# A fused two-block transformer kernel: mLSTM order, first feed-forward features, expert buffers and one set of modulation loads

## The reference

```
first_block:  cond = silu(c) @ w_ada + b_ada              # shifts, scales, gates ("modulation")
  layer 0:    x = layer_norm(ALPHA*x + gate * mlstm_layer(modulate(x)))          "ln00"
              x = layer_norm(ALPHA*x + gate * moe_ffn(modulate(x)))              "ln01"
  layer 1:    x = layer_norm(ALPHA*x + gate * moba_layer(modulate(x), kv))       "ln10"
              x = layer_norm(ALPHA*x + gate * moe_ffn(modulate(x)))              "ln11"
second_block, twice:
              x = x + 0.5 * swiglu(rms_norm(x) * ffn1)    # width 2816; "f10", "f11"
              x = x + three mixers of rms_norm(x) * mix, gated and merged
              x = x + 0.5 * swiglu(rms_norm(x) * ffn2)    # "f20", "f21"
mlstm_layer:  4 heads of 512; per head q, k, v, masked q.k weights, sum over values, a group norm
              over the head (mean, variance), then (norm*gn_g + skip*xc) * silu(z), then @ w_out
moe_ffn:      16 experts of 1024 x 512 (gate, up) and 512 x 1024 (down), top 2 for each token
```

## Time and profile before

| | us |
|---|---|
| median of 3 runs (2419.46 to 2423.87) | 2422.51 |
| the profiled execution | 2422.62 |
| its span, from the first to the last instruction | 2420.8 |
| PE busy | 2277.3 (94%) |
| PE weight loads busy | 1743.2 (72%) |
| DVE busy | 1247.5 (52%) |
| ACT busy | 949.8 (39%) |
| mean granted TensorE clock | 0.977 |

### The profile page before, as it was taken

How to read it: one execution, slowest core, us unless ns; L and a number is a source line. 1 busy time by engine, 2 the same in 40 slices (tenths; PEclk the granted TensorE clock), 3 DMA queues, 4 the chain that set the end, 5 groups by cost and what they waited for, 6 DMA issues and landing times.

```text
span 2420.8 us, 33290 instructions
## 1 busy us (share of the span) xinstructions
PE 2277.3 (94%) x12894; PEld 1743.2 (72%) x12894; DVE 1247.5 (52%) x2278; ACT 949.8 (39%) x1702; POOL 113.8 (5%) x96
## 2 busy tenths in 40 slices
PE   6999998998999899979999889999999999899999
PEld 4877774444477444458878679888788886698887
DVE  4624535111322511157764666777677636666776
ACT  2532202111222211145443665554554446645553
POOL 1000000000000000000005200000000052000000
PEclk8999999999999999989999999999999999999999
DMA  9975439999821899946653424466566534154663
GB/s 353 320 238 211 156 116 407 428 430 428 310 105 70 370 428 430 428 142 208 187 180 135 147 70 174 132 208 187 151 209 183 193 107 174 36 176 139 209 182 95
DMA packets 310253, 535.63 MB, mean 221 GB/s; under 512 B 14894, under 2 KB 200944, under 8 KB 296304
## 3 DMA queue, kind: packets, MB, share of 16 engines
q1 hardware_dynamic: 309180, 532.61, 61.1%
q10 hardware_dynamic: 948, 1.28, 0.2%
HBM read 532.81 MB, written 1.05 MB: 221 GB/s over the span
## 4 chain that ended last, share of the span: by engine, by line
PE 83%; DVE 8%; ACT 3%; DMA 3%; issue 2%; SPq 1%; POOL 0%; ACTq 0%; DVEq 0%
PE bank L593 15%; PE bank L1045 14%; PE bank L874 13%; PE yacc L908 9%; PE bank L879 7%; PE bank L577 5%; PE yacc L788 2%; PE yacc L610 2%; PE bank L628 2%; PE bank L1260 1%; PE yacc L1057 1%; PE bank L657 1%; PE yacc L1204 1%; PE bank L985 1%; PE bank L750 1%
## 5 line engine op out<-in xcount | busy, mean ns | idle before, releaser
L1424 ACT ACTIVATE arena<-bank 128x256 f32<-128x256 f32 (+3 forms) x382 | 146.3, 407 | 588.1 <-PE bank L593 127.4
L874 PE MATMUL bank<-h_split,w_hi 128*128 128x512 f32 x1408 | 351.7, 392 | 0.0
L2316 DVE TENSOR_TENSOR w_lo<-wring,w_hi 128x1024 fp32r<-128x1024 f32 x264 | 307.4, 1219 | 10.7 <-ACT w_hi L1644 10.7
L1644 ACT ACTIVATE w_hi<-wring 128x1024 fp32r<-128x1024 f32 x264 | 277.4, 1056 | 49.0 <-PE yacc L908 49.0
L874 PEld LDWEIGHTS bank<-h_split,w_hi 128*128 128x128 f32 x1408 | 259.1, 189 | 49.8
L879 PEld LDWEIGHTS bank<-h_split,w_lo 128*128 128x128 f32 x1408 | 192.9, 191 | 19.1 <-DVE h_split L2358 4.5
L879 PE MATMUL bank<-h_split,w_lo 128*128 128x256 f32 x1408 | 199.1, 284 | 3.9 <-DVE h_split L2358 3.9
L2906 POOL TENSOR_TENSOR wx_lo<-wring,wx_hi 128x1024 fp32r<-128x1024 f32 x42 | 107.3, 2557 | 1935.5 <-ACT wx_hi L1464 1935.5
L1045 PE MATMUL bank<-wring,arena 128*64 128x512 f32 x768 | 172.3, 603 | 15.1 <-issue 7.9
L1045 PE MATMUL bank<-arena 128*64 128x512 f32 x672 | 171.5, 604 | 9.4 <-issue 5.5
L1656 ACT ACTIVATE H<-bank 128x256 f32<-128x256 f32 x176 | 67.2, 382 | 251.4 <-PE bank L879 250.4
(11 more groups left out here) (403 smaller groups left out, 3813.9 us busy)
## 6 DMA issues: line engine op xcount, KB each, us to landing
wring<-in_ffn_w_in SPq DMA_DIRECT2D x176, 512.0 KB
wring<-in_w_ada SPq DMA_DIRECT2D x28, 2048.0 KB
wring<-in_ffn_w_out SPq DMA_DIRECT2D x88, 512.0 KB
wring<-in_w_in SPq DMA_DIRECT2D x20, 2048.0 KB
wring<-in_moe_w_gate SPq DMA_DIRECT2D x16, 2048.0 KB, 21.8
wring<-in_moe_w_up SPq DMA_DIRECT2D x16, 2048.0 KB, 20.8
wring<-in_moe_w_down SPq DMA_DIRECT2D x16, 2048.0 KB, 22.3
arena<-in_moe_w_down SPq DMA_DIRECT2D x12, 2048.0 KB, 20.0
```

The source lines that it names most:

```text
L874: return mm(b[:, :], r(w_hi[:, j % 2, g, c * HB:(c + 1) * HB]), r(h_split[:, c, :, :].rearrange("p a t -> p (a t)")), start=start, stop=st ...
L1424: ins = f(dst, bank_of(name)[0:dst.shape[0], 0:T] if src is None else src, func, **kw)
L1644: f(w_hi[:, j % 2, part, :].bitcast(F32R), wring[:, u % WSLOTS, part * DC * HB:(part + 1) * DC * HB], ACT.Copy).then_inc(w_hi_ready[part], 1)
L2316: tt(w_lo[:, j % 2, part, :].bitcast(F32R), wring[:, (u0 + j) % WSLOTS, part * DC * HB:(part + 1) * DC * HB], w_hi[:, j % 2, part, :], ALU ...
```

## The change

Four edits, none of which changes what is computed.

1. **mLSTM order.** On DVE, `mlstm_out(h-1)` is split. Its first two operations stay, as `mlstm_scaled`; skip, gain and gate move behind the drains of `mbc` and `mS`. On PE, `head_out(2)` is split: three of its eight output chunks go ahead of head 3's variance sum.
2. **First feed-forward's features.** f10 no longer goes through token-major form. In ln11 ACT writes the high part of h straight from X, with a bias of ffn1 * ln_b, ahead of each chunk's own offset; DVE makes the rest from X. PE's transposes of X to token form lie between the first matmuls of `up` and go into `yacc`; ACT copies them to `Xt` afterwards. The first weights' rounding moves ahead of ln11's squares on ACT, and between centring and reciprocal on DVE. `scale_rows` moves behind the second `up`.
3. **Experts' buffers.** Slots 0 to 3 are now the arena's, 4 to 7 the ring's, and SP issues units in the order of use. For the first MoE, two of ln00's modulation pieces are loaded ahead of unit 0 and two ahead of unit 2.
4. **ln01's modulation pieces** are loaded into the arena places of units that have been used, with a semaphore each, and no longer into the ring.

```diff
+MOE_AHEAD = MOE_SLOTS - WSLOTS
 def moe_slot(l, n):
-            if j < WSLOTS:
-                return (wring[:, (moe_first[l][0] + j) % WSLOTS, 0:size],)
-            if j - WSLOTS < len(MOE_EXTRA):
-                return (arena[:, MOE_EXTRA[j - WSLOTS]:MOE_EXTRA[j - WSLOTS] + size],)
-            return arena[:, MOE_SPLIT:MOE_SPLIT + size // 2], expert_half[:, :]
+            if j < len(MOE_EXTRA):
+                return (arena[:, MOE_EXTRA[j]:MOE_EXTRA[j] + size],)
+            if j < MOE_AHEAD:
+                return arena[:, MOE_SPLIT:MOE_SPLIT + size // 2], expert_half[:, :]
+            return (wring[:, (moe_first[l][0] + j - MOE_AHEAD) % WSLOTS, 0:size],)
...
 SP, def moe(l, units):
-                        if n < MOE_SLOTS:
-                            n = (n + WSLOTS) % MOE_SLOTS
-                        if n < WSLOTS:
-                            sp.wait_ge(*moe_first[l][1][n])
+                        for a in units.get(n, []):
+                            ada(a)
+                        if n < MOE_AHEAD:
+                            sp.wait_ge(*arena_left[l][n])
                         elif n < MOE_SLOTS:
-                            sp.wait_ge(*arena_left[l][n - WSLOTS])
+                            sp.wait_ge(*moe_first[l][1][n - MOE_AHEAD])
...
-            for a in ADA_NORM["ln00"]:
-                ada(a)
-            moe(0)
-            for a in ADA_NORM["ln01"][0:3]:
-                ada(a)
+            moe(0, {0: ADA_NORM["ln00"][0:2], 2: ADA_NORM["ln00"][2:4]})
+            for i in range(3):
+                sp.wait_ge(*moe_unit_used(0, PAIRS * PAIR_UNITS - MOE_SLOTS + i))
+                ada_extra(i)
             for n in range(2):
                 load(f"bv{n}", (A["b_w_kv"][:, D + n * 512:D + (n + 1) * 512], DC))
-                if n == 0:
-                    ada(ADA_NORM["ln01"][3])
+            sp.wait_ge(*full(f"ada{ADA_NORM['ln01'][0]}"))
+            ada_extra(3)
...
 PE, end of moe(l):
                 for j in range(WSLOTS):
-                    freed[j - WSLOTS] = moe_unit_used(l, range(j, PAIRS * PAIR_UNITS, MOE_SLOTS)[-1])
+                    freed[j - WSLOTS] = moe_unit_used(l, range(MOE_AHEAD + j, PAIRS * PAIR_UNITS, MOE_SLOTS)[-1])
...
 PE, after the heads:
             mlstm_mean(NH - 1)
+            head_out(2, 0, 3)
             mlstm_var(NH - 1)
-            for h in range(2, NH):
-                head_out(h)
+            head_out(2, 3)
+            head_out(3)
...
 PE, up(0, 0) of f10:
                                 left(c, c == 0, False)
+                                if g == 0 and tag == "f10":
+                                    turn_tokens(c)
...
                 up(0, 0, True)
-                scale_rows()
+                if tag != "f10":
+                    scale_rows()
                 for j in range(BODY):
                     up(0, j + 1)
+                    if tag == "f10" and j == 0:
+                        scale_rows()
                     down(0, j, first=(j == 0))
...
 ACT:
+                        if dst is X:
+                            f(h_split[:, k, 0, :].bitcast(F32R), X[:, k, :], ACT.Identity, scale=vec("ffn1", k),
+                              bias=lnv[:, 0, k:k + 1]).then_inc(h_hi_ready.sem, 1)
                         f(dst[:, k, :], dst[:, k, :], ACT.Identity, bias=offset).then_inc(ready.sem, 1)
...
             moe(1)
+            swiglu("f10", 0, "ffn1", 0, 0, True)
             layer_norm("ln11", [(X, x_ready)])
-            act.wait_ge(*full("xt3"))
+            act.wait_ge(xt_turned, 4)
+            act.wait_ge(h_lo_ready.sem, h_lo_ready.upto("act", DC))
...
 DVE, head h:
                 if h > 0:
-                    mlstm_out(h - 1)
+                    mlstm_scaled(h - 1)
                 dve.wait_ge(*full(f"mbc{h}"))
...
                 moved(f"mS{h}", ...)
+                if h > 0:
+                    mlstm_out(h - 1)
...
 DVE, layer_norm, after the centring:
+                if between:
+                    between()
...
-            ffn_weights(0)
+            layer_norm("ln11", 1, 1, between=lambda: ffn_weights(0))
```

More of the change, by code:

```diff
@@ L263, in build @@
         c_ready = sem("c_ready")
+        ada_landed = [sem(f"ada_landed{i}") for i in range(4)]
         h_ready = Signal(sem("h_ready"))
@@ L659, in ada_unit @@
                 filled(f"ada{n}", last)
[L660 removed]
+                if not extra:
+                    used_by(f"ada{n}")
             def ada_turn(n):
@@ L781, in _, with head_out @@
                 filled(f"mbc{h}", mm(b[:, T:2 * T], ident[0:NH, h:h + 1].broadcast_to([NH, P]), lrow[6][:, :], start=True, stop=True))
[L782 to L786, removed]
+            def head_out(h, first=0, end=DC):
+                if first == 0:
+                    weights(f"a_w_out{h}")
+                    pe.wait_ge(head_ready.sem, head_ready.upto("pe"))
+                u = tags.index(f"a_w_out{h}")
+                w = wring[:, u % WSLOTS, 0:DHC * D].rearrange("p (k n) -> p k n", k=DHC)
+                for m in range(first, end):
                     for k in range(DHC):
@@ L1667, in step @@
                         high(i, j + 1, 2)
-                for j in range(2):
-                    for part in range(2):
-                        high(0, j, part)
-                for kk in range(DC // 2):
+                if ahead or tag != "f10":
+                    for j in range(2):
+                        for part in range(2):
+                            high(0, j, part)
+                if ahead:
+                    return
+                for kk in range(0 if tag == "f10" else DC // 2):
                     act.wait_ge(*full(f"{tag}.x{kk}"))
@@ L2353, in swiglu @@
                     return
-                for kk in range(DC // 2):
+                if tag == "f10":
+                    for k in range(DC):
+                        dve.wait_ge(h_hi_ready.sem, h_hi_ready.upto("dve"))
+                        dve.wait_ge(x_ready.sem, x_ready.upto("dve"))
+                        stt(h_split[:, k, 1, :].bitcast(F32R), X[:, k, :], vec(gain, l * DC + k), h_split[:, k, 0, :],
+                            ALU.mult, ALU.subtract).then_inc(h_lo_ready.sem, 1)
+                    for part in range(2):
+                        low(0, 1, part)
+                for kk in range(0 if tag == "f10" else DC // 2):
                     dve.wait_ge(h_hi_ready.sem, h_hi_ready.upto("dve", 2))
@@ L2361, in swiglu @@
                 token_rstd()
-                for j in range(early, 2):
+                for j in range(2 if tag == "f10" else early, 2):
                     for part in range(2):
@@ L2713, in swiglu, with moe @@
                 nxt[0] += STEPS
-            def moe(l):
-                assert nxt[0] == moe_first[l][0]
+            def moe(l, units):
+                assert nxt[0] + sum(len(u) for u in units.values()) == moe_first[l][0]
                 mats = [A[f"moe_w_{name}"][l].rearrange("e (p k) n -> p e k n", p=P) for name in ("gate", "up", "down")]
```

68 lines of the change are left out of this document (43 added, 25 removed).

## The result

The changed kernel took 2402.02 us (median of 4, 2400.19 to 2405.31), the kernel before 2421.86 us in the same comparison: ratio 0.9914, 95% interval 0.9902 to 0.9926, that is 20.8 us faster (17.9 to 23.7). The prediction was 2399.0 us in a range of 2393 to 2407, and 23.6 us faster. The profiled execution took 2402.46 us with a span of 2400.6.

What follows compares the result with a forecast made beforehand. In the first MoE the stream of expert weights was taken as the limit, its end following unit 8's issue. 21.0 (15.7 mLSTM, 5.3 numbering) + 2.6 (f10) = 23.6 us off 2422.62 gave 2399.0, range 2393 to 2407.

Steps and rivals of the forecast that it cites:

- Heads: mLSTM: PE's waits of 2.41 and 2.53 us at heads 2 and 3 and slow records behind them go, 8.6 us.
- All signs that were named: mLSTM: no idle time ahead of PE's q products of heads 2 and 3, nor ahead of the variance sum.
- Variance: mLSTM: the 4.78 us wait ahead of head 3's variance sum goes, with slow records: 7.1 us.
- the 0.4 us to spare: mLSTM: PE's remaining head 2 records and the sum cover head 3's gate, 8.93 us behind the sum, with 0.4 us left.
- Expert units: First MoE: unit 8 issued at 386.0 instead of 407.00, 21.0 us: 15.7 from the mLSTM, 5.3 from the numbering.
- unit 8's issue dates the end of the stage: First MoE: pair 7's up product follows unit 8's issue by 189.75 us, so moving one moves the other.
- Second MoE and ln01's pieces: Second MoE's first units issued at the same events, ln01's modulation pieces at the same uses: 0 us each.
- f10's start: Start of f10: first down 4.4 us earlier, less 1.8 for slow records behind a 5.8 us gap: 2.6 us.
- f10 gives all: Rival at f10's start: no gap, 21.0 + 8.8 = 29.8 us faster, 2392.8; chance 0.09.
- PE's ten us: Start of f10: up(0,0) is done at 1067.9, ten us earlier.
- the single chances: Forecast 0.55, head's wait 0.13, f10 loses 0.12, f10 gives all 0.09, late weights 0.05 and 0.02, no change 0.04.
- First weights of f10 too late: Rival: f10's later first load delays ACT ahead of ln11's squares, 7.0 us lost, 2406.0, chance 0.05; slower overall, 0.02.

Runs made afterwards that it cites:

- a_heads: The kernel before with only DVE's part of the mLSTM edit (skip, gain and gate behind the drains): 0.9952, 11.6 us faster.
- both single edits: The kernel before with the mLSTM edit alone (0.9923), and with the experts' numbering and ln01's modulation pieces in the arena alone (0.9974).
- half_release: scale_first with units 8 and 9 of both MoEs loaded in halves, the first halves issued halfway through pair 0's gate product: 0.9857, 34.7 us faster than before.
- filled_gap: The changed kernel with 24 unneeded products in PE's idle stretch ahead of f10's first down: 0.9891, 26.4 us faster than the kernel before.
- scale_first: The changed kernel with scale_rows put back behind up(0,0), ahead of up(0,1), in f10: 0.9869, 31.8 us faster than the kernel before.
- a_f10: The kernel before with the edit of f10's start alone: 0.9997 (0.9988 to 1.0006).
- ada_ring: The changed kernel with ln01's four modulation pieces back in the ring: 0.9907 against the kernel before.
- short_down: The changed kernel loading only half the rows of most down units from unit 8 on, computing something else: 0.9833, 40.5 us faster than the kernel before.

## Why the prediction was right, and where it was off

**Heads, 8.6 us: right.** All signs that were named are there, and in a_heads' trace the variance sum came 8.7 us earlier. The time itself, 11.6 us faster (7.5 to 15.5), is too wide to tell this from 9.5.

**Variance, 7.1 us: right, as a difference.** 7.5 or 6.6 in the traces, by where it is taken; the 0.4 us to spare was enough, since nothing waits in head 3's place.

**Expert units, 21.0 us: right in its parts.** Pair 0's gate product without a DMA wait at 380.73 (forecast 378.9; with the late start of 1.6 that is 379.1 against 378.9), unit 8 at 387.84 (386.0), 190.05 us to pair 7's up product (189.75). Net of the start unit 8 moved by 20.8. The mLSTM's 15.7 and the numbering's 5.3 measured 15.6 and 5.6 apart. But the reason given was too strong: "unit 8's issue dates the end of the stage". It does while all of pair 0 moves with it, as it did in before, after and both single edits (189.75 to 190.12 us). half_release moved the stream's start alone by 3.4 us, and the end followed by 0.4 to 0.5, about an eighth.

**Second MoE and ln01's pieces, 0: right.** From unit 8 to pair 7's up product 190.06 and 189.89 us in the second MoE; the ring's pieces cost the same as the arena's.

**f10's start, 2.6 us: the mechanism was right, two sizes were not.** The copy and `down` were forecast 4.4 us earlier (net of the rest); they came 3.7 earlier, mainly because a pair of ACT's rounding and offset takes 0.89 to 0.91 us (1034.73 - 1033.82 = 0.91) and not 2 x 0.41, which over eight pairs is 0.6 us. The slow stretch was taken as 1.8 us, from gaps of 2.4 to 4.8 us; behind 5.78 us it was 2.44 (5.25 for 2.81). 3.7 - 2.5 = 1.2 us. I took 1.8 although the gap was longer than any that had given it. For the longest wait, 4.78 us, give more: the 0.61 of the variance sum and the 1.74 behind it are 2.35 us, and the clock of that sum was 0.50, where behind the waits of 2.41 and 2.53 us it was 0.76 and 0.70 over the 24 and 16 records. So not only part of the records can be slow. By "TensorE: Matmul & The Clock Gate" in the Trainium skill, section "Why this matters for your kernels", the gap was to be avoided. filled_gap and scale_first agree, with 2.4 us for the clock. The prediction said so and still passed over the larger thing: the 5.8 us of wait itself was of the edit's making, and putting one call back was worth 8.0 us in f10. (One rival's sum has a step that isn't there: "f10 gives all" keeps "PE's ten us" but adds 8.8. And the single chances add up to 0.94 for faster and 0.02 for slower, not 0.93 and 0.03.)

**First weights of f10 too late: did not happen.** ACT's roundings ended with 3.6 us of idle time left ahead of ln11's squares, whose distance to ln10 changed by 0.7 us.

**The total.** Expected 23.6, measured 20.8 (17.9 to 23.7). The trace's 20.2 are 23.6 less the start's 1.6, less 1.4 of f10, plus 1.1 of the mLSTM's and the first MoE's more, less 1.5 for the attention, the second MoE, the mixer and the rest together, in which PE's instructions did not change. None of these was in the prediction, and their signs differ: that the total came within 3 us is in part luck. The start alone varied between 158.7 and 162.0 us in the twelve traces. The -1.65 us of the attention and the +1.9 of the mixer are records that ran slower or faster, below.

## What to carry to other kernels

Before a producer is moved behind a block of work "since nobody needs it yet", follow its consumer's whole chain on the other engines: `scale_rows` took 0.4 us of PE, and moving it 5.5 us back left 5.8 us of ACT and DVE uncovered and the clock down behind it. In a stage where transfers are the limit, measure how much PE's own work leaves to be gained (here 8 to 10 us a stage, though 29 us of transfer were left out) and whether slots and not only the start hold the stream, before buying an earlier start. And where a kernel's span is compared between two traces, take it apart at the same instructions: 1 to 2 us a stretch can differ where nothing was changed.

## What the hardware showed that I had not expected

Stretches in which PE's instructions are the same differed by up to 3 us from trace to trace, and where I looked into them they did so with the place at which the granted clock falls. ln01's to ln10's mean sum, before and after (columns as in the earlier trace rows):

```profile
621.42:790.70 169.28, 163.66 (x725) 114.69 (x721) 54.23 (x175) 48.64 (x159) 0.00 (x0) 0.99 0.39 142
```

```profile
600.93:768.56 167.63, 162.01 (x725) 113.52 (x722) 54.20 (x175) 48.63 (x159) 0.00 (x0) 1.00 0.39 145
```

The same 725 records of PE took 163.66 and 162.01 us. In before the clock was 0.79 in the eight us from 152 us on (by a view of stretches of 8 us), in after 1.00 throughout, with the same 8.00 us of PE busy there and 6.67 of 8 in the stretch ahead in both. In all twelve traces (the ten runs above, before and after) this stretch took either 167.6 or 169.3 us and nothing between. By "TensorE: Matmul & The Clock Gate" in the Trainium skill, section "What's actually happening", the chip judges activity over periods that run freely and don't start with the kernel. The two values fit this, but no run here tests it.

f10's end to the mixer's second sum of squares took 166.5 to 168.7 us. The changed kernel lost 1.9 us there and f10's edit alone 1.6, in the same places. The clearest is the stretch from 102 to 114 us behind f10's end, before and after:

```profile
1359.44:1371.44 12.00, 9.66 (x83) 9.05 (x81) 1.05 (x3) 10.04 (x18) 2.38 (x1) 1.00 0.48 175
```

```profile
1336.74:1348.74 12.00, 9.66 (x71) 9.31 (x70) 1.05 (x3) 8.89 (x17) 0.68 (x1) 0.86 0.51 176
```

The clock was 1.00 before and 0.86 after; in the same 9.66 us of busy time PE got through 83 records before and 71 after, and f10's edit alone shows 71 and 0.86 as well. Elsewhere it is the other way round: in the six us from 54 us on the clock was 0.67 before and 0.88 after. This may be more than chance. The four traces with the gap ahead of f10's first `down` (after, a_f10, ada_ring, short_down) took 168.3 to 168.7 us here, the eight others 166.5 to 168.0. So part of what f10's edit gained may be lost again in the mixer, which would fit the 0.9997 of a_f10 and the 11.0 us of scale_first, where f10 gave 8.0. Against it, filled_gap has no idle stretch there and yet took 167.5, 0.7 more than before. No run here separates this from the place where the clock happens to fall.

The last 993 us differed too, between 991.7 and 994.8. So stretches with unchanged PE instructions differ by 1 to 3 us between traces, in either direction, and below that no single trace tells what an edit is worth.
